# A routed expert layer: block 0's first layer in plain fp32 products, its rows fetched by a list of their own

## What is computed

```python
h = rmsnorm(x, g_ffn)
logits_g = h @ w_grp;  g_idx = argmax(logits_g)
le = (h @ w_exp)[g_idx];  top_v, top_i = top_k(le, 2)
expert = g_idx * 8 + top_i
weight = softmax(logits_g)[g_idx] * softmax(top_v)
# for each block of up to 128 (token, choice) pairs of one expert:
a = silu(xb @ w1[e]) * (xb @ w3[e])
y = (a @ w2[e]) * w
x = x + sum of y over a token's two pairs;  out = rmsnorm(x, g_final)
```

## Time and profile before

| | |
|---|---|
| median of 3 runs | 1020.4 us (1018.98 to 1021.54) |
| the profiled execution | 1020.05 us, span 1018.4 us |
| TensorE (PE) busy | 964.2 us, 95% |
| VectorE (DVE) busy | 740.6 us, 73% |
| ScalarE (ACT) busy | 443.8 us, 44% |
| GpSimd (POOL) busy | 222.4 us, 22% |
| DMA, mean over the span | 187 GB/s |

### The profile page before, as it was taken

One profiled execution on the slowest core, in us unless ns is written; L12 is line 12 of the kernel. 1 busy time (PEld: TensorE's weight loads), 2 busy tenths in 40 slices (PEclk: granted clock), 3 DMA queues, 4 the chain that ended last, 5 costly groups with the idle time before them and its releaser, 6 DMA issues.

```text
span 1018.4 us, 16148 instructions
## 1 busy us (share of the span) xinstructions
PE 964.2 (95%) x5356; PEld 835.3 (82%) x5357; DVE 740.6 (73%) x1631; ACT 443.8 (44%) x739; POOL 222.4 (22%) x227
## 2 busy tenths in 40 slices
PE   6999999999999999999998999969999999999970
PEld 6998898988889888898886888858888888888850
DVE  5965466755678556685558666589999999999955
ACT  6621122111221212212123112148988898898864
POOL 0001220012200122001220110031444444444220
PEclk9999999999999999999999999979999999999995
DMA  9511105111051110512027332389999999999838
GB/s 315 181 42 54 47 17 178 38 53 39 24 175 41 53 35 28 173 36 83 30 85 257 141 149 97 117 327 408 391 396 394 391 400 388 392 394 388 332 49 333
DMA packets 74771, 190.21 MB, mean 187 GB/s; under 512 B 12663, under 2 KB 47587, under 8 KB 62275
## 3 DMA queue, kind: packets, MB, share of 16 engines
q1 hardware_dynamic: 61099, 159.07, 41.3%
q0 software_dynamic: 13456, 29.69, 10.0%
q10 hardware_dynamic: 144, 0.52, 0.2%
HBM read 167.95 MB, written 38.68 MB: 203 GB/s over the span
## 4 chain that ended last, share of the span: by engine, by line
PE 85%; DVE 6%; DMA 4%; ACT 2%; issue 2%; SPq 1%; POOL 0%; DVEq 0%; POOLq 0%; ACTq 0%
PE bank L2018 18%; PE bank L888 11%; PE bank L890 11%; PE bank L889 11%; PE bank L2019 9%; PE bank L919 8%; PE bank L1059 3%; PE bank L2007 1%; PE bank L959 1%; PE bank L2033 1%; PE bank L2041 1%; PE bank L2029 1%; DMA raw<-in_w_in_dram 1%; PE bank L2037 1%; DVE x L1471 1%
## 5 line engine op out<-in xcount | busy, mean ns | idle before, releaser
L1349 DVE TENSOR_TENSOR w_lo<-w,w_hi 128x1024 fp32r<-128x1024 f32 x128 | 150.5, 1218 | 0.3
L777 ACT ACTIVATE w_hi<-w 128x1024 fp32r<-128x1024 f32 x128 | 129.6, 1069 | 3.4 <-PE bank L890 3.4
L888 PE MATMUL bank<-w_hi,xT_hi 128*128 128x512 f32 x256 | 102.9, 402 | 2.3 <-issue 2.3
L2018 PE MATMUL bank<-wvg_hi,hT_hi 128*128 128x512 f32 x256 | 104.3, 408 | 0.0
L2018 PE MATMUL bank<-wvg_lo,hT_hi 128*128 128x512 f32 x256 | 100.9, 394 | 0.0
L2018 PE MATMUL bank<-wvg_hi,hT_lo 128*128 128x512 f32 x256 | 100.6, 393 | 0.0
L890 PE MATMUL bank<-w_hi,xT_lo 128*128 128x512 f32 x256 | 100.2, 392 | 0.0
L1825 ACT ACTIVATE v<-bank 128x256 f32<-128x256 f32 x32 | 12.3, 383 | 201.2 <-PE bank L2019 201.2
L889 PE MATMUL bank<-w_lo,xT_hi 128*128 128x512 f32 x256 | 99.7, 390 | 0.0
L2373 POOL TENSOR_TENSOR mixed<-onorm,pgate 128x256 f32<-128x256 f32 x36 | 38.9, 1082 | 273.2 <-DVE onorm L2189 273.2
L888 PE MATMUL bank<-hT_hi,wuqk_hi 128*128 128x344 f32 x288 | 94.1, 327 | 0.1
(11 more groups left out here) (281 smaller groups left out, 2393.2 us busy)
## 6 DMA issues: line engine op xcount, KB each, us to landing
w<-in_w_dram SPq DMA_DIRECT2D x96, 1024.0 KB, 17.7
raw<-in_w_in_dram SPq DMA_DIRECT2D x57, 256.0 KB, 3.3
mixed_d<-mixed POOLq DMA_DIRECT2D x32, 128.0 KB, 2.2
sample_state<-in_state_ret_dram SPq DMA_DIRECT2D x16, 256.0 KB, 3.8
out_dram<-sample_state SPq DMA_DIRECT2D x16, 256.0 KB, 3.6
mixed_in<-mixed_d SPq DMA_DIRECT2D x8, 512.0 KB, 4.3
x_again<-in_x_prompt_dram SPq DMA_DIRECT2D x8, 512.0 KB, 3.4
h_d<-h POOLq DMA_DIRECT2D x8, 512.0 KB, 3.0
```

The source lines that it names most:

```text
L777: act.activation(hi, whole_w, ACT.Copy).then_inc(S["up_hi"], 1)
L888: pe.matmul(out, lhs[0], rhs[0], start=first, stop=False)
L1349: dve.tensor_tensor(lo, whole_w, hi, ALU.subtract).then_inc(S["up_lo"], 1)
L2018: g = pe.matmul(gates, x[xi], wvg[wi][:, 1:3, k, :], start=first, stop=last)
```

## The change

- TensorE gets a second list, `first_listing`: behind `listing(CH - 1)` it sums only the eight prompt tiles, into bank 3. VectorE takes column 0 (expert 0, so block 0), makes `pair_first` and `tok_first` of it, and raises `routed` for the first time. Both stand ahead of the ninth tile's `router` and `norm`.
- GpSimd fetches block 0's prompt rows by `tok_first` from `h2_d` into `junk_f`, which it has set to zero at tile 3; slots without a prompt row stay zero. This fetch stands ahead of the ninth tile's two stores, and it waits for the eight prompt tiles' rows to be stored. It raises `xg_in[0]` in place of the gather of block 0, which is gone.
- VectorE makes `sample_slot` after the ninth tile's `places`: one row for each sample, with a one at the slot of block 0 that the sample has, if any.
- TensorE's `first_rows` takes the place of `x_over(0, 0, 1)`: for each of the eight column groups a product of the fetched rows with the identity, and one that adds the sample rows of `h2` by `sample_slot`.
- ScalarE copies banks 0 and 1 to `xT_first`, fp32 and unsplit. `up(0)` is eight plain fp32 products of 512 columns with the loaded weights. Block 0's `up_high`, `up_low`, `x_high` and `x_low` are gone; `up_high` of block 1, pieces 0 to 2, moves ahead to where block 0's was.
- The gather of block 2 waits until `first_rows` is through.

The core of the diff:

```diff
+        xT_first = nc.alloc_sbuf_tensor_at("xT_first", [P, KT, P], F32, offset=rx.where["xT_hi0"])
...
             act.wait_ge(S["w_mm"], after(NT))
-            for q in range(UPS):
-                up_high(0, 0, 0, q)
+            act.sem_inc(S["up_hi"], UPS)
+            for q in range(3):
+                up_high(1, 1, 0, q)
...
-            x_high(0, 0)
+            for n in range(2):
+                act.wait_ge(S["xt2_mm"], after(n + 1))
+                act.activation(xT_first[:, 4 * n:4 * n + 4, :].rearrange("p k n -> p (k n)"), banks[n][:, :], ACT.Copy)\
+                    .then_inc(S["xT_hi_ev"], 1)
...
+            def first_listing():
+
+                for u in range(CH):
+                    for j in range(2):
+                        for a in range(2):
+                            mm = pe.matmul(banks[3][:, 0:NE], slot_hot[:, u, j, :], planes[:, u, a, j, :],
+                                           start=(u + j + a == 0), stop=(u == CH - 1 and j + a == 2))
+                mm.then_inc(S["list_mm"], 1)
...
             x2_over(CH, 1)
             listing(CH - 1)
+            first_listing()
             router(CH)
...
             def up(b, slot, s2, ks=range(KT)):
                 pe.wait_ge(S["a_done"], after(b - 1))
                 out = banks[2 + s2][:, :].rearrange("p (j f) -> p j f", j=2)
+                if is_first(b, 1):
+                    pe.wait_ge(w13_in[0], 32)
+                    for k in ks:
+                        if k % 4 == 0:
+                            pe.wait_ge(S["xT_hi_ev"], after(k // 4 + 1))
+                        pe.matmul(out, xT_first[:, k, :], w13[0][:, :, k, :], start=(k == 0), stop=(k == KT - 1))\
+                            .then_inc(S["up_used"], 1)
+                    return
...
-            x_over(0, 0, 1)
+            def first_rows():
+
+                pe.wait_ge(xg_in[0], 16)
+                pe.wait_ge(S["routed"], after(2))
+                rows = junk_f[:, :].rearrange("p (d k) -> p k d", k=KT)
+                samples = h2[CH % 2][:, :].rearrange("p (d k) -> p k d", k=KT)
+                for n in range(2):
+                    for j in range(4):
+                        out = banks[n][:, j * P:(j + 1) * P]
+                        pe.matmul(out, rows[:, 4 * n + j, :], ident, start=True, stop=False)
+                        mm = pe.matmul(out, samples[0:NB, 4 * n + j, :], sample_slot[0:NB, :], start=False, stop=True)
+                    mm.then_inc(S["xt2_mm"], 1)
+
+            first_rows()
...
             x2_second_half(CH)
+            dve.wait_ge(S["list_mm"], after(1))
+            do(dve.tensor_scalar(pair_first[:, :], banks[3][:, 0:1], 4096.0, None, ALU.add))
+            dve.tensor_scalar(tok_first[:, :], pair_first[:, :], 1, None, ALU.logical_shift_right)\
+                .then_inc(S["routed"], 1)
             norm(CH)
             picks(CH)
             places(CH)
-
-            dve.wait_ge(S["list_mm"], after(1))
+            dve.wait_ge(S["hot_done"], after(NT))
+            do(dve.tensor_scalar(sample_slot[0:NB, :], slot_hot[0:NB, CH, 0, :], chosen[0:NB, 2 * CH, 0:1], None, ALU.mult))
...
-            for q in range(UPS):
-                up_low(0, 0, q)
+            dve.sem_inc(S["up_lo"], UPS)
+            dve.sem_inc(S["xT_lo_ev"], 2)
             pair_weights()
-            x_low(0, 0)
             weight_planes()
...
+                elif t == CH:
+                    pool.wait_ge(S["icol_done"], after(2))
+                    for i in range(2):
+                        pool.wait_ge(h2_out[i], 16 * CH // 2)
+                    pool.wait_ge(S["routed"], after(1))
+                    pool.indirect_dma_start(
+                        out=junk_f[:, :], out_offset=None, in_=h2_d[0:SEQ, :],
+                        in_offset=bass.IndirectOffsetOnAxis(ap=tok_first[:, :], axis=0),
+                        bounds_check=last_prompt, oob_is_err=False).then_inc(xg_in[0], 16)
                 if t == CH:
+                    pool.wait_ge(S["h2_done"], after(NT))
                     pool.dma_start(h2_d[SEQ:NTOK, :], h2[s][0:NB, :]).then_inc(h2_out[s], 16)
...
+                elif is_first(b, 3) and b == 2:
+                    pool.wait_ge(S["xt2_mm"], after(2))
```

More of the change, by code:

```diff
@@ L344, in step_kernel @@
         no_row = rc.place("no_row", [P, 1], I32)
+        pair_first = rc.place("pair_first", [P, 1], I32)
+        tok_first = rc.place("tok_first", [P, 1], I32)
+        sample_slot = rc.place("sample_slot", [P, P], F32)
+        assert rc.at <= whole.end
         SS, MS, RS = 0, 9, 18
@@ L773, in up_high @@
                     act.wait_ge(w13_in[s % SLOTS], 32 * uses(s, g))
-                if not is_first(b, 1):
+                if not is_first(b, 2):
                     act.wait_ge(S["up_used"], after(KT * (b - 1) + 2 * q + 2))
@@ L830, in step_m @@
                     return
-                for q in range(3):
-                    up_high(b + 1, s + 1, g, q)
+                if not is_first(b, 1):
+                    for q in range(3):
+                        up_high(b + 1, s + 1, g, q)
                 sigmoid(b, s % 2)
@@ L1299, in stage_c_dve @@
             places(CH)
-            dve.wait_ge(S["list_mm"], after(1))
+            dve.wait_ge(S["hot_done"], after(NT))
+            do(dve.tensor_scalar(sample_slot[0:NB, :], slot_hot[0:NB, CH, 0, :], chosen[0:NB, 2 * CH, 0:1], None, ALU.mult))
+            dve.scalar_tensor_tensor(out=sample_slot[0:NB, :], in0=slot_hot[0:NB, CH, 1, :],
+                                     scalar=chosen[0:NB, 2 * CH + 1, 0:1], in1=sample_slot[0:NB, :],
+                                     op0=ALU.mult, op1=ALU.add).then_inc(S["routed"], 1)
+            dve.wait_ge(S["list_mm"], after(2))
             do(dve.tensor_scalar(idx_pair[:, 0:NE].rearrange("p (e g) -> p e g", g=4),
@@ L1339, in slot_weights @@
             def slot_weights():
-                dve.wait_ge(S["list_mm"], after(2))
+                dve.wait_ge(S["list_mm"], after(3))
                 dve.tensor_reduce(slot_w[:, 0:NE].rearrange("p (e g) -> p e g", g=4),
@@ L1486, in stage_c_pool @@
             pool.reg_mov(last_row, NTOK - 1)
+            last_prompt = pool.alloc_register("last_prompt")
+            pool.reg_mov(last_prompt, SEQ - 1)
             for t in range(NT):
                 s = t % 2
-                pool.wait_ge(S["h2_done"], after(t + 1))
+                if t < CH:
+                    pool.wait_ge(S["h2_done"], after(t + 1))
                 if t == 2:
@@ L1497, in stage_c_pool @@
                         bounds_check=SEQ - 1, oob_is_err=False).then_inc(x2_out, 16)
+                elif t == 3:
+                    pool.wait_ge(x2_out, 16 * 4)
+                    pool.memset(junk_f[:, :], 0.0).then_inc(S["icol_done"], 1)
+                elif t == CH:
[7 more added lines that the diff above has]
+                        bounds_check=last_prompt, oob_is_err=False).then_inc(xg_in[0], 16)
                 if t == CH:
+                    pool.wait_ge(S["h2_done"], after(NT))
                     pool.dma_start(h2_d[SEQ:NTOK, :], h2[s][0:NB, :]).then_inc(h2_out[s], 16)
@@ L1506, in stage_c_pool @@
             pool.wait_ge(S["x2_done"], after(2 * NT))
-            pool.wait_ge(S["routed"], after(1))
+            pool.wait_ge(S["routed"], after(3))
             def gather(b, slot, used, index):
@@ L1521, in gather @@
                     pool.tensor_copy(index, idx_tok[:, bass.ds(b, 1)]).then_inc(S["icol_done"], 1)
-                    pool.wait_ge(S["icol_done"], after(b - SLOTS + 2))
+                    pool.wait_ge(S["icol_done"], after(b - SLOTS + 3))
                     carried(pool, "pool")
@@ L1546, in step_m @@
             def step_m(b, s, g):
-                gather(b, s % SLOTS, uses(s, g), icol[s][:, :])
+                if not is_first(b, 1):
+                    gather(b, s % SLOTS, uses(s, g), icol[s][:, :])
                 if not is_first(b, SLOTS):
```

## The result

The change made the kernel slower by 14.0 us, where the forecast was 3.0.

A forecast was written before the change was run, and what follows sets the result against it. TensorE was taken to set the pace. Idle products' end to first layer's end, 8.39 us, became 10.40 (+2.01); with +1.04 for the listing, +3.05 us: median 1023.4, forecast's own range 1022.2 to 1025.0, whole range 1020.6 to 1025.8.

The forecast's parts named there:

- Turning by products: Turning of block 0's rows: sixteen plain fp32 products at 0.22 us, 3.52 us, replace eight transposes of 0.88 in all.
- The rule of the Trainium skill: Load of the stationary operand in the turning: goes by columns, not contraction rows, so the full 3.52 us holds.
- First layer in eight products: Block 0's first layer: eight plain fp32 products of 512 columns at 0.86 us take 6.88 us instead of 5.73.
- (c): Rival, in the turning: the 8-row products are nearly free; +1.3 us, 1021.7 us; chance 0.08.
- The listing ahead of the norm: Before the last tile's norm: 32 listing products and VectorE's index instructions delay routing and the idle products; +1.04 us.
- (d): Rival, before the turning: the fetch lands late, at 683.1, and TensorE waits 1.0 us more; 1024.4 us; chance 0.08.
- (e): Rival, before block 2's turning: block 2's gather is late; at a landing time of 16 us, 2 us; 1025.5 us; chance 0.08.
- (a): Rival, in the expert blocks: weight loads set the pace; filling a DMA gap ends the kernel 3.3 us sooner, 1017.1; chance 0.06.
- (b): Rival, before the turning: the clock doesn't drop, the idle products take 2.55 us; +0.5 us, 1020.9 us; chance 0.07.
- The 2.73 behind the first layer: From block 0's first layer to block 1's first product: the same chain after the change, kept at 2.75 us.
- The remark on four passes: Block 0's first layer: true fp32 as four passes at 0.239 us would take 7.6 us, making the sum +3.8.
- "without a gap, in 3.5 us": Sign in the changed trace: the turning's plain products follow the idle products without a gap and take 3.5 us.

The follow-up runs named there:

- the all-rows kernel: The changed kernel, with the sample products taking all 128 rows of both operands (120 more, zero in the slot matrix), stride kept: 1027.36 us, 1.0075 of before.
- the grouped: The changed kernel, with each bank's four products of fetched rows first, then its four of samples; only the order changes: 1031.45 us, 1.0115 of before.

## Why the prediction was wrong

The direction was right and the size was not: +14.0 us instead of +3.0, a time of 1034.9 where the range ended at 1025.8.

**What failed: "Turning by products", 3.52 us.** It measured 11.51. The row it rests on the earlier trace rows has neighbouring values as its stationary operand, and the products around it have its own depth. I took it for the 8-row products because they differed "only in depth", and said nothing of the stride, which the diff shows in the `rearrange`. Both mattered. By the experiments the 11.51 come from 3.58 (all rows, neighbours), +3.9 for the stride (7.52 with all rows), +3.2 for turns of 128 and 8 rows (16 x 0.67 = 10.7 at full clock), and the rest, 0.8, for the low clock. So one change of depth costs about 0.2 us, with or without the stride (0.42 - 0.22, and 0.67 - 0.475). The prices are consistent with one picture: where depth stays, loads overlap the products and only the slower of them counts (0.22, or 0.465 at the stride); where it changes, load and product add up (2 x 0.11 + 0.22 = 0.44 against 0.42 measured; 2 x 0.235 + 0.22 = 0.69 against 0.67). The loads' idle time in the changed kernel is seen; that load and product run one after the other is inferred from these sums, not seen as such.

The rule of the Trainium skill that I weighed there (page "TensorE: Matmul & The Clock Gate", section "LDWEIGHTS (loading the stationary operand)": a load goes by columns, not by rows) holds for the load: in the changed kernel a listed load of 8 rows takes 317 ns and one of 128 rows 323. It doesn't give the price of the pair, since it says nothing of what happens when the depth changes.

**What was missing: the clock.** "First layer in eight products", 6.88, was right at full clock: 6.87 in each of the three kernels with products for the turning that kept it. That the clock would stay full had gone unsaid. The earlier trace rows made me ask about the idle products alone; I gave each later term at 2.4 GHz. The 9.66 measured are 2.8 us more. No rival had a fall of the clock in it, and (c), nearly free 8-row products, bounded their cost from the wrong side.

**The sum, mended.** Forecast +3.05; stride +3.9, depth +3.2, clock +0.8 in the turning and +2.8 in the layer make +13.75, against +14.0 for the medians and +13.60 at block 1's first product. The sum is made of the profiles' pieces, of one execution each.

**What held.** The listing ahead of the norm: +0.84 at the end of the idle products, which ended at 681.91 against 682.1 forecast; the norm began at 670.17 against 670.37. The listing itself started 0.14 earlier in this execution (668.72, before 668.86), so it cost 0.98 against the 1.04 forecast. The fetched rows were no bottleneck: the fetch, issued at 671.1, took 8.3 us to land, about 679.4, just behind the 676 to 679 taken as likelier. The turning stood behind the idle products until 681.91, so an earlier fetch could gain nothing, and (d) did not happen. (e) did not either, as no TensorE wait stands before block 2's turning. (a) would have shown as an end 3.3 us earlier; the pace from block 1 on is the old one but for the 0.65 us above. (b) failed: the idle products took 5.07 us. The 2.73 behind the first layer against 2.75 is as forecast. The remark on four passes (page "FP8 and Floating Point Precision", section "TensorE Precision Notes", of the Trainium skill) gave 7.6 us by the 0.239 of a single-pass product, and 6.87 were measured. The trace has two records a product and doesn't show the passes; if they are four, one is 0.215 here (6.87 / 32, an estimate), so it would be the price of one pass that was too high.

The text itself had named the test: a stream of plain products "without a gap, in 3.5 us". There was no gap, and 11.5 us.

## What to carry to other kernels

A price from a row holds only for the same operand layout, the same depth and the same neighbours in the queue: before moving one over, compare the access pattern of the stationary operand and what stands before and behind it. Between full-depth products, join a few extra rows with a full-depth product padded by zeros rather than a product of 8 rows: here that took the turning from 11.5 to 7.5 us and kept the clock. Where such products lowered the clock here they stood right behind a rise of it; in the middle of a long stretch at full clock nothing was tried. And fetching earlier what wasn't waited for gains nothing, while the listing for it cost 1 us; ask first what the fetch's reader itself is behind.

## What the runs showed of the hardware

- **Stride of the stationary operand.** Plain fp32 products of 128 columns take 0.22 us with neighbouring values and 0.465 to 0.475 at a step of 32 bytes; a listed load takes 192 against 334 ns. Eight transposes of rows with that same step took 0.88 in all, 0.11 each, without such a price, and their listed load is 188 ns in the kernel before. Why they are spared wasn't tried.
- **Change of depth.** Products of 128 and 8 rows by turns take 0.42 (neighbours) and 0.67 us (stride) each; of one depth in a row 0.22 and 0.44 to 0.475. That is 0.2 us for a change.
- **The clock under a busy engine.** In the three kernels that mixed in 8-row products at full clock it fell to 0.50 (1.2 GHz) although TensorE was busy all along, and in the one that began at 0.50 it stayed there for 12.4 us. With 128-row products alone, at the same stride, it stayed at 1.00 (2.4 GHz) for sixteen products, 7.5 us. Where it was at 0.50 it rose again only 4.6 to 5.7 us into the first layer. What in the short products it is that the clock follows stays open. Between the changed and the all-rows kernel the depth differs, and with it the pace (0.67 against 0.475); between the grouped and the all-rows kernel the depth and the order, at nearly one pace.
- **Idle products.** The same six took 4.0 to 5.3 us from one profiled execution to another (4.03, 4.08, 5.07, 5.25, 5.31), as the clock rose sooner or later: 2.6 us after their start in the run without samples, 4.7 us in the changed kernel, and only behind them in the one with neighbouring channels. Where the turning waits for nothing else, some 1.3 us of an execution's time are decided there.
